# Banded attention: the low part of the meta keys' P made on POOL ahead of the turn, beside P in the turned slice; the weights' low parts in two halves

## What is computed

```python
s_meta = einsum('bcqgrd,bmgd->bcqgrm', qc, k_meta) * scale       # 16 columns
s_band = einsum('bcqgrd,bckgd->bcqgrk', qc, kb) * scale           # own chunk and 2 before it
p = sink_softmax(concatenate([s_meta, where(valid, s_band, -inf)]), sinks)
o = einsum('bcqgrm,bmgd->bcqgrd', p[..., :16], v_meta) + einsum('bcqgrk,bckgd->bcqgrd', p[..., 16:], vb)
```

## Time and profile before

| | us |
|---|---|
| median of 3 runs | 1664.82 (1663.62 to 1667.56) |
| the profiled execution | 1662.88 |
| its span | 1661.1 |
| banded attention, PE's view | 400 to 556 |
| PE busy | 1638.8 (99%) |
| DVE, ACT, POOL busy | 1082.1, 774.6, 346.6 (65%, 47%, 21%) |

### The profile page before, as it was taken

How to read it: one execution, slowest core, us unless ns; L and a number is a source line. 1 busy time by engine, 2 the same in 40 slices (tenths; PEclk the granted TensorE clock), 3 DMA queues, 4 the chain that set the end, 5 groups by cost and what they waited for, 6 DMA issues and landing times.

```text
span 1661.1 us, 27363 instructions
## 1 busy us (share of the span) xinstructions
PE 1638.8 (99%) x9476; PEld 1484.0 (89%) x9476; DVE 1082.1 (65%) x2320; ACT 774.6 (47%) x1630; POOL 346.6 (21%) x503
## 2 busy tenths in 40 slices
PE   8999999999999999999999999999999999999998
PEld 8999999999999989989988998888888888888886
DVE  7566666635999544364445597778887668774744
ACT  6487887865778433342234333222222434343521
POOL 1323333234322322234533120000000000000242
PEclk9999999999999999999999999999999999999999
DMA  5222212322222554563334332344443764444541
GB/s 181 80 62 58 62 48 60 98 81 69 68 68 58 189 164 162 171 218 124 133 127 127 115 108 97 119 145 134 143 145 131 247 208 116 127 152 123 190 165 76
DMA packets 164347, 205.43 MB, mean 124 GB/s; under 512 B 16168, under 2 KB 113256, under 8 KB 164240
## 3 DMA queue, kind: packets, MB, share of 16 engines
q1 hardware_dynamic: 164240, 204.04, 38.3%
HBM read 144.88 MB, written 57.32 MB: 122 GB/s over the span
## 4 chain that ended last, share of the span: by engine, by line
PE 81%; DVE 9%; issue 4%; ACT 3%; POOL 2%; DMA 1%; SPq 0%; DVEq 0%; POOLq 0%; ACTq 0%
PE gb L543 8%; PE gb L2400 5%; PE sc L3283 5%; PE gb L3283 5%; PE gb L2935 4%; PE gb L2771 4%; PE sc L2935 4%; PE tp L2935 4%; PE tp L3283 4%; PE gb L993 3%; PE gb L994 3%; PE gb L995 3%; PE tp L842 3%; PE sc L2559 3%; PE tp L2559 3%
## 5 line engine op out<-in xcount | busy, mean ns | idle before, releaser
L513 POOL TENSOR_TENSOR wl<-raw,wh 128x256 fp32r<-128x256 f32 x168 | 125.1, 776 | 260.7 <-ACT wh L498 173.5
L993 PE MATMUL gb<-Xh,wh 128*128 128x384 f32 (+1 forms) x504 | 173.1, 343 | 0.0
L994 PE MATMUL gb<-Xh,wl 128*128 128x384 f32 (+1 forms) x504 | 170.9, 339 | 0.0
L995 PE MATMUL gb<-Xl,wh 128*128 128x384 f32 (+1 forms) x504 | 170.9, 339 | 0.0
L3407 POOL TENSOR_TENSOR wl<-raw,wh 128x1024 fp32r<-128x1024 f32 x2 | 5.3, 2628 | 559.6 <-ACT wh L3398 559.6
L543 PE MATMUL gb<-Xh,wh 128*128 128x384 f32 (+1 forms) x288 | 104.0, 361 | 0.0
L543 PE MATMUL gb<-Xh,wl 128*128 128x384 f32 (+1 forms) x288 | 97.6, 339 | 0.0
L543 PE MATMUL gb<-Xl,wh 128*128 128x384 f32 (+1 forms) x288 | 97.4, 338 | 0.0
L993 PEld LDWEIGHTS gb<-Xh,wh 128*128 128x128 f32 x504 | 94.9, 188 | 0.4
L994 PEld LDWEIGHTS gb<-Xh,wl 128*128 128x128 f32 x504 | 94.9, 188 | 0.1
L995 PEld LDWEIGHTS gb<-Xl,wh 128*128 128x128 f32 x504 | 94.8, 188 | 0.0
(11 more groups left out here) (569 smaller groups left out, 4764.5 us busy)
## 6 DMA issues: line engine op xcount, KB each, us to landing
zr<-u_scr SPq DMA_DIRECT2D x91, 256.0 KB, 3.0
raw<-in_w_in SPq DMA_DIRECT2D x70, 256.0 KB, 3.3
u_scr<-ustore SPq DMA_DIRECT2D x26, 576.0 KB, 4.5
u_scr<-ustore SPq DMA_DIRECT2D x13, 768.0 KB, 3.2
sig_scr<-sig SPq DMA_DIRECT2D x16, 576.0 KB, 3.1
raw<-in_w_up SPq DMA_DIRECT2D x36, 256.0 KB, 4.5
kc<-in_cache_fox_k SPq DMA_DIRECT2D x8, 1024.0 KB, 5.7
vc<-in_cache_fox_v SPq DMA_DIRECT2D x8, 1024.0 KB, 7.6
```

The source lines that it names most:

```text
L513: last = nc.gpsimd.tensor_tensor(wl[U.slot][:, q], raw[U.slot][:, q], wh[U.slot][:, q].bitcast(F32), ALU.subtract)
L993: nc.tensor.matmul(bank[:, 0:x1 - x0], wh[U.slot][:, ws], Xh3[:, k, x0:x1], start=(k == 0), stop=False)
L994: nc.tensor.matmul(bank[:, 0:x1 - x0], wl[U.slot][:, ws], Xh3[:, k, x0:x1], start=False, stop=False)
L995: last = nc.tensor.matmul(bank[:, 0:x1 - x0], wh[U.slot][:, ws], Xl3[:, k, x0:x1], start=False, stop=(k == KT - 1))
```

## The change

- `es[x]` gets `ES0 = 32` columns in front. P of the item stands from column 32 on; columns 0 to 15 take its low part, and 16 to 31 are zero (two memsets before the stage). The first turned slice is columns 0 to 127, so the low part comes out in rows 0 to 15 and P's meta columns in rows 32 to 47, both by the one turn. The values' rows serve both.
- DVE's instruction above goes. In its place POOL makes, for each item, a copy of the 16 scaled columns in the shortened form (`mh`), and the subtraction.
- PE's turn waits for that subtraction, besides the scale. The value products no longer wait for `meta_lo`.
- POOL's list: the pair of item s-1 stands first in step s. The low part of a weight unit is made in two halves of two instructions, one and two steps after ACT's second half; the last unit's follows the loop.
- ACT's first half of a high part no longer raises a semaphore (nobody waited for it).

```diff
@@ -48,6 +48,7 @@
 MB = META + P
+ES0 = 32
@@ -249,12 +250,13 @@
         lfq = sb("lfq", [8, NT], ctx=A2k)
-        es = [sb(f"es{x}", [P, 296], ctx=A2k) for x in range(2)]
+        es = [sb(f"es{x}", [P, ES0 + 296], ctx=A2k) for x in range(2)]
         vball = sb("vball", [P, 4 * P], ctx=A2k)
...
         lfT = sb("lfT", [P, 80], ctx=A2k)
-        sb("before_keys", [P, 432], ctx=A2k)
+        mh = [sb(f"mh{x}", [P, META], F32R, A2k) for x in range(2)]
+        sb("before_keys", [P, 336], ctx=A2k)
@@ -413,7 +415,7 @@
         raw_full = [sem(f"raw_full{s}") for s in range(2)]
-        w_hi, w_lo, w_half = sem("w_hi"), sem("w_lo"), sem("w_half")
+        w_hi, w_lo, meta_hi = sem("w_hi"), sem("w_lo"), sem("meta_hi")
         gemm_done = sem("gemm_done")
@@ -502,17 +504,21 @@
                 act.wait_ge(gemm_done, U.n * 3 - 3)
-            nc.scalar.activation(wh[U.slot][:, 512 * x:512 * x + 512], raw[U.slot][:, 512 * x:512 * x + 512],
-                                 ACT.Copy).then_inc((w_half, w_hi)[x], 1)
-
-        def lo(pool, U):
-
-            pool.wait_ge(w_hi, U.n + 1)
-            for x in range(4):
+            half = nc.scalar.activation(wh[U.slot][:, 512 * x:512 * x + 512], raw[U.slot][:, 512 * x:512 * x + 512],
+                                        ACT.Copy)
+            if x == 1:
+                half.then_inc(w_hi, 1)
+
+        def lo(pool, U, part=range(4)):
+
+            if part[0] == 0:
+                pool.wait_ge(w_hi, U.n + 1)
+            for x in part:
                 q = slice(256 * x, 256 * x + 256)
...
                                                ALU.subtract)
-            last.then_inc(w_lo, 1)
+            if part[-1] == 3:
+                last.then_inc(w_lo, 1)
@@ -1673,6 +1679,8 @@
             pool.wait_ge(pv_done, GROUPS)
+            for x in range(2):
+                nc.gpsimd.memset(es[x][:, 0:ES0], 0.0).then_inc(meta_hi, 1)
             for h in range(2):
@@ -1771,21 +1779,33 @@
                 act.wait_ge(tp_full, SWA_RB + n - 1)
-            nc.scalar.activation(es[h][:, 0:b], u[h][:, 0:b], ACT.Exp, bias=mx[:, m:m + 1], scale=-1.0,
+            nc.scalar.activation(es[h][:, ES0:ES0 + b], u[h][:, 0:b], ACT.Exp, bias=mx[:, m:m + 1], scale=-1.0,
                                  accum_out=ssum[:, n % 4:n % 4 + 1]).then_inc(p_done, 1)
...
 
-            ps = es[n % 2][:, 0:swa_width(n % 16 // 2)]
+            ps = es[n % 2][:, ES0:ES0 + swa_width(n % 16 // 2)]
             v.wait_ge(sum_inv, ITEMS + n + 1)
...
 
+        def swa_meta_pool(pool, n):
+
+            x = n % 2
+            pool.wait_ge(p_scaled, ITEMS + n + 1)
+            if n >= 2:
+                pool.wait_ge(meta_lo, n - 1)
+            nc.gpsimd.tensor_copy(mh[x][:, :], es[x][:, ES0:ES0 + META]).then_inc(meta_hi, 1)
+            pool.wait_ge(meta_hi, n + 3)
+            nc.gpsimd.tensor_tensor(es[x][:, 0:META], es[x][:, ES0:ES0 + META], mh[x][:, :].bitcast(F32),
+                                    ALU.subtract).then_inc(meta_lo, 1)
+
         def swa_slices(i):
-            return (0, META) if i == 0 else (0, META, MB + META)
+            return (0, ES0 + META) if i == 0 else (0, ES0 + META, ES0 + MB + META)
 
...
             pe.wait_ge(p_scaled, ITEMS + n + 1)
+            pe.wait_ge(meta_lo, n + 1)
             round_fill(pe, Round(SWA_RB + n), [es[n % 2][:, c:c + P] for c in swa_slices(n % 16 // 2)])
@@ -1806,8 +1826,6 @@
             v.wait_ge(tp_hi, HI_SWA + n + 1)
-            nc.vector.tensor_tensor(PTh3[32:32 + META, a, x:x + P], rbank[R.slot][0:META, 0:P],
-                                    PTh3[0:META, a, x:x + P].bitcast(F32), ALU.subtract).then_inc(meta_lo, 1)
             c = 2 * (n // 2 % 3)
@@ -1820,7 +1838,6 @@
                 rounds_read(pe, [Round(SWA_PRE + 1), Round(SWA_PRE + 2)])
-            pe.wait_ge(meta_lo, 2 * G + 2)
             pe.wait_ge(o_done, GROUPS + (G if G == GROUPS - 1 else G - G % 2))
@@ -1945,15 +1962,19 @@
             for s in range(STEPS):
+                if 0 <= s - 1 < ITEMS:
+                    swa_meta_pool(pool, s - 1)
                 if 1 <= s < ITEMS - 1 and (s + 1) % 16 < 2:
...
                         rope_pool(pool, Unit(m), c, 3 + 3 * u_ + c, nA[u_ % 2])
-                for m, x in SWA_HI[s]:
-                    if x == 1:
-                        lo(pool, Unit(m))
+                for d in (2, 1):
+                    for m, x in SWA_HI[s - d] if s >= d else ():
+                        if x == 1:
+                            lo(pool, Unit(m), range(2 * d - 2, 2 * d))
+            lo(pool, Unit(SWA_FILL_UNITS[-1] + 2))
```

## The result

The changed kernel takes 1675.51 us (median; 1674.85 to 1678.39) against 1664.8 before. By these medians it is 10.7 us or 0.64% slower; the measured ratio is 1.0074, with a 95% interval of 1.0062 to 1.0085, which makes the loss 12.3 us (10.3 to 14.2).

A forecast was written before the change was run, and what follows sets the result against it. The prediction took PE, 99% busy, to bound the kernel, so only its waits could be won. Its terms, -6.8 + 1.5 + 19.7 = +14.4 us, gave 1677.3 for the profiled execution and 1679.2 for the median, range 1670 to 1690.

The forecast's parts named there:

- What bounds the stage: Banded attention, 400 to 556 us: PE is 99% busy overall; its 6.8 us of waits for DVE's scale are the most winnable.
- DVE's relief: DVE loses 64 low-part instructions, 18.0 us, and no longer sets the pace; nearly all of PE's 6.8 us goes.
- The pair's price: POOL's copy and subtraction before each turn: 0.68 us from end of scale to turn, where 0.05 stood.
- Rival B: The pair takes 1.2 us or more, so items with little slack wait too: about 1689 us; chance 10%.
- The 1.5 us of small waits: Turns of the thinnest items and steps where ACT is behind still wait a little: 1.5 us, bounds 0 and 6.8.
- The rope stalls: Pairs stand behind nine ropes in POOL's queue, which wait for DMAs, so PE's turns wait: 19.7 us, bounds 15.0 and 26.
- the upper bound of 26: Upper bound of the nine rope waits' sum, with ACT's copy late as at 490 us and the dearer pair.
- the five ordinary ropes: Ropes e = 6, 20, 38, 41 hold PE's turn 0.8 us each, e = 23 1.25: 4.5 us.
- rival C: PE's clock falls to 1.2 GHz behind each of four stalls of 3 to 5 us: +9 us, 1688; chance 8%.
- Rival A: POOL's queue is no obstacle and DVE's relief is won, less 1.5: -5.3 us, 1659.5; chance 8%.
- Rival D: Stalls come smaller, because DVE's and ACT's relief brings copy and DMA forward: 1664 to 1672 us; chance 8%.

The follow-up runs named there:

- rope_late: The changed kernel with each chunk's rope one step later in POOL's list, behind one more pair: 1667.34 us, ratio 1.0023 to the kernel before.
- load_late: The changed kernel with SyncE's load of the weights after next issued two steps later, behind the rope's DMAs: 1667.59 us, ratio 1.0021 to the kernel before.
- spread2: The changed kernel with POOL's list rewritten (pair first, rope and low-part pieces spread, loads behind rope DMAs), then pieces moved to other steps: 1659.72 us, ratio 0.9977.
- whole_low: The changed kernel with the weights' low part in one piece in its old step, not in halves: 1686.19 us, ratio 1.0132 to the kernel before.
- spread: The changed kernel with POOL's list rewritten: pair first, rope instructions and low-part halves in separate steps, loads behind rope DMAs: 1661.54 us, ratio 0.9983.
- pair_aside: The changed kernel with POOL's pair working on other columns into an unread tile, the turn not waiting, meta keys' low part left out: 1658.98 us, ratio 0.997.

## Why the prediction was right, point by point

- **What bounds the stage**: right. DVE's relief alone is worth 5.5 us (forecast 6.8). The stage got longer by 10.85 us, where some 14 were forecast.
- **The pair's price**: forecast 0.68 us from scale to turn. The lines by form, POOL, of the changed kernel:

```profile
L1799 POOL TENSOR_TENSOR es<-es,mh 128x16 f32<-128x16 f32 x64 | 14.5, 227 | 5.1
L1797 POOL CAST mh<-es 128x16 fp32r<-128x16 f32 x64 | 12.9, 201 | 70.7 <-DVE es L1789 70.7
```

  The copy is as in the earlier trace rows; the subtraction takes 0.23, not 0.30, so a straight line through two wide forms overstates a narrow one here. From end of scale to end of pair 0.56 us pass (446.73 to 447.29) and some 0.07 to the turn: 0.63. Rival B (a dear pair) is out. The 1.5 us of small waits came as 0.2 (items 29 and 45).
- **The rope stalls**: the mechanism is shown by the timelines and by `rope_late` and `load_late`; the sizes were off. Forecast and measured: items 3 and 5, 3.4 and 2.8 against 3.1 (turn at 412.01 for 408.87) and 1.7. Item 5 is less because the rope that ended at 418.55 in the earlier trace rows ended at 417.41; the one slow DMA of the trace of before, 5 us where the others took 3.9, did not come back. Item 19, 4.7 against 3.3: the half low part ended 2.8 us after PE's step began, not 3.4 to 4.5, since the scale ahead of it is no longer late (it ended 0.8 us after the step's start, and 2.2 before). Item 37, 4.3 against 4.2. Three sizes are loose in the forecast itself: from its own rows item 3 comes to 411.41 + 0.7 - 408.87 = 3.2 and not 3.4, item 37 to 4.2 and not 4.3, and the upper bound of 26 is not added up.
- **The term that was mis-sized most**: the five ordinary ropes, 4.5 us in the forecast, 1.4 measured (0.2, 0, 0.9, 0, 0.3). The forecast measured one of them from the start of PE's step, with PE running. Three of the five (e = 6, 20, 38) follow a stall, and while PE stood, ACT did the copy for the next rope. ACT's timeline of the changed kernel:

```profile
416.80 0.49 ACT L1090 ACTIVATE u<-gb 128x384 f32<-128x384 f32 x1
...
451.24 0.49 ACT L1090 ACTIVATE u<-gb 128x384 f32<-128x384 f32 x1
...
498.36 0.49 ACT L1090 ACTIVATE u<-gb 128x384 f32<-128x384 f32 x1
```

  PE's steps began at 418.00, 454.11 and 501.88. So the copy was made 1.2 to 3.5 us before the point from which the forecast counts 0.8 us until its start. The rope of e = 6 ended 6.4 us after 418.00, instead of 6.8 to 7.3, and that of e = 20 ended 6.3 us after 454.11. One stall pays for part of the next. At e = 20 and 38 PE was also at half clock, which made the three steps longer (8.4 us, 454.11 to 462.48); in `load_late`, with the clock up, the turns of these two ropes wait 0.34 us and nothing. Of the other two, e = 23 has the copy 0.4 us after the step's start for 0.8 before, since ACT is no longer late and waits for PE there, and its turn waits 0.9 for the forecast's 1.25.
- **What was missing**: the turn of item 0. The forecast had PE covered there; the four instructions of the low part before the loop ended at 404.18, after PE's groups of steps 0 and 1, and the first turn waited 1.6 us for its pair, standing at 404.70 for 403.10. POOL's and PEld's timelines:

```profile
401.19 2.99 POOL L518 TENSOR_TENSOR wl<-raw,wh 128x256 fp32r<-128x256 f32 x4
404.13 0.20 POOL L1797 CAST mh<-es 128x16 fp32r<-128x16 f32 x1
404.41 0.23 POOL L1799 TENSOR_TENSOR es<-es,mh 128x16 f32<-128x16 f32 x1
```
```profile
404.70 0.20 PEld L848 LDWEIGHTS gb<-ident,es 128*128 128x128 f32 x2 [1.64 <-issue]
```

  It added little to the total: the turn of item 3 is set by its rope and came 3.1 us late in all, with the 1.6 of item 0 in it.
- **The clock** (rival C): it came at two of the four long stalls and cost 3.4 us, where the rival had 9. Little of it was hidden in the waits of the ordinary ropes behind it: at most the 0.34 us that item 22 waits in `load_late`.
- **Rival A** (POOL's queue is no obstacle) fell in the change and is what `spread2` makes of it: the gain is there once nothing slow stands ahead of the pair. **Rival D** had a mechanism that was at work: the relief of DVE and ACT did bring copies and DMAs forward (items 19 and 25). But it took some 2 us off the stalls, and the time stayed above D's 1672.

Two errors ran against each other: stalls 7 us too high (21.2 with the small waits, 14.2 measured), and 3.4 us of clock left out. So the mechanism was right, and that the time came within 3.7 us of the forecast is in part luck.

## What to carry to other kernels

Before an engine with much idle time gets work that the busiest engine waits for, list all that stands ahead of that work in its queue, with what each entry itself waits for: here 45 busy us of 152 hid nine DMA waits and eight blocks of 3 us. Follow the queues one further, since the wait of SyncE for POOL's low part, free before, cost 8 us (`load_late`), 3.4 of them by the clock. Put the awaited work first and cut what is between into pieces shorter than the slack; that turned +10.7 us into -3.9 us by the medians, with the same instructions. And don't add up stalls one by one: each gives the other engines time to get ahead with what the next one would wait for.

## What the runs showed of the hardware

- PE's granted clock fell from 1.00 to 0.50, its level of 1.2 GHz, when work had begun again behind waits of 3.3 and 4.2 us, and rose again under that work. Behind the waits of 1.6 to 1.75 us in the same stage it stayed at 1.00. The Trainium skill (TensorE: Matmul & The Clock Gate, "HAM oscillation") says that idle gaps in mid-kernel bring the clock down; the trace agrees at these two places.
- The length of a wait alone did not decide it. In `whole_low` the clock fell behind waits of 2.75 and 3.4 us and stayed at 1.00 behind one of 3.2 us, as the table by stretch shows behind the wait of 2.75, which ended at 427.49, and that of 3.2, which ended at 473.87:

```profile
428.00:429.00 1.00, 1.00 (x5) 1.00 (x5) 0.21 (x1) 0.49 (x1) 0.00 (x0) 0.50 0.78 176
...
475.00:476.00 1.00, 1.00 (x10) 1.00 (x9) 0.97 (x4) 0.61 (x2) 0.00 (x0) 1.00 1.05 303
```

- Two-input work of DVE was stretched beside POOL: in `spread` line 1727 took 0.80 us beside POOL's instruction of 447.55, and 0.42 in most places. The Trainium skill (SBUF — State Buffer, "Who interferes with whom") says that such pairs exclude each other; the trace agrees here, and `pair_aside` shows that 128 short POOL instructions right behind the scale don't add up to a cost here.
